# Three 1 MB weight loads in the row stage, each issued in two parts of 120 and 8 partitions

## The reference, cut to what matters

```python
def peer_ffn(x, w_query, sub_keys, expert_u, expert_v):
    def block(xb):                                   # 128 tokens
        q = (xb @ w_query).reshape(128, 8, 2, 128)
        sc = jnp.einsum('thpd,hpkd->thpk', q, sub_keys)
        s_top, i_top = lax.top_k(sc, 16)             # best keys of each half
        ...                                          # best 16 of the 256 sums -> eidx, g = softmax(best)
        u = jnp.take(expert_u, eidx, axis=0)
        h = jax.nn.gelu(jnp.einsum('thkd,td->thk', u, xb))
        vv = jnp.take(expert_v, eidx, axis=0)
        return jnp.einsum('thk,thkd->td', g * h, vv)
```

## Time and profile before

| | |
|---|---|
| median of 3 runs | 1161.68 us (1161.17 to 1161.84) |
| the profiled execution's own time | 1159.69 us |
| its span, first to last instruction | 1157.9 us |
| TensorE busy | 1051.7 us (91%) |
| VectorE busy | 834.9 us (72%) |
| ScalarE busy | 390.7 us (34%) |
| GpSimd busy | 269.4 us (23%) |
| DMA, whole span | 371.86 MB, mean 321 GB/s |
| granted TensorE clock, mean | 0.994 |

### The profile page before, as it was taken

One profiled execution on the slowest core, in us unless ns is written; L12 is line 12 of the kernel. 1 busy time (PEld: TensorE's weight loads), 2 busy tenths in 40 slices (PEclk: granted clock), 3 DMA queues, 4 the chain that ended last, 5 costly groups with the idle time before them and its releaser, 6 DMA issues.

```text
span 1157.9 us, 11980 instructions
## 1 busy us (share of the span) xinstructions
PE 1051.7 (91%) x4108; PEld 665.7 (57%) x4108; DVE 834.9 (72%) x1747; ACT 390.7 (34%) x724; POOL 269.4 (23%) x261
## 2 busy tenths in 40 slices
PE   8999899998998778798877777889999999999998
PEld 6888464454454333244322222359878778888886
DVE  5788878778877768787787776764565496777743
ACT  7664312211220111311121012044765555444432
POOL 0002444434444334433433343400000000000000
PEclk9999999999999989999999999999999999999999
DMA  9847999999999999999999999977533454555540
GB/s 351 337 167 302 423 421 421 421 421 421 420 420 423 420 422 421 421 414 420 411 421 421 405 423 414 423 282 275 177 138 124 161 193 157 192 183 189 192 164 36
DMA packets 55531, 371.86 MB, mean 321 GB/s; under 512 B 6192, under 2 KB 7344, under 8 KB 12080
## 3 DMA queue, kind: packets, MB, share of 16 engines
q0 software_dynamic: 36864, 268.45, 56.0%
q1 hardware_dynamic: 18608, 102.65, 24.4%
HBM read 370.03 MB, written 1.05 MB: 320 GB/s over the span
## 4 chain that ended last, share of the span: by engine, by line
PE 58%; DMA 30%; DVE 8%; issue 3%; ACT 1%; POOL 1%; SPq 0%; DVEq 0%; POOLq 0%; ACTq 0%
DMA uv<-in_peer_uv,eidx 30%; PE bank L2232 13%; PE bank L1931 9%; PE bank L1933 8%; PE bank L1932 8%; PE bank L2406 6%; PE bank L2003 4%; DVE uv L1548 4%; PE bank L2405 3%; PE bank L1902 1%; DVE diag L1562 1%; PE bank L2121 1%; DMA wraw<-in_in1a 1%; POOL uv L721 1%; DVE xn L1770 0%
## 5 line engine op out<-in xcount | busy, mean ns | idle before, releaser
L2232 PE MATMUL bank<-uv,diag 128*128 128x512 f32 x1024 | 491.8, 609 | 92.7 <-DVE diag L1562 91.3
L1548 DVE SCALAR_TENSOR_TENSOR uv<-uv,xn 128x1024 f32<-128x1024 f32 x256 | 313.6, 1225 | 134.6 <-DMA uv<-in_peer_uv,eidx 132.9
L2232 PEld LDWEIGHTS bank<-uv,diag 128*128 128x128 f32 x1024 | 180.3, 191 | 368.4 <-issue 366.2
L721 POOL DMA_INDIRECT uv<-in_peer_uv,eidx x256 | 269.0, 1051 | 480.0 <-PE bank L2232 358.9
L1265 DVE TENSOR_TENSOR w_lo<-wraw,w_hi 128x2048 fp32r<-128x2048 f32 x69 | 157.8, 2290 | 102.4 <-ACT w_hi L797 102.3
L1008 ACT ACTIVATE chosen<-chosen 128x1 f32<-128x1 f32 x256 | 51.8, 203 | 504.9 <-DVE uv L1548 504.7
L797 ACT CAST w_hi<-wraw 128x2048 fp32r<-128x2048 f32 x69 | 131.5, 1908 | 125.5 <-PE bank L1933 63.1
L2406 PE MATMUL bank<-nT_both,w_hi 128*128 128x512 f32 x320 | 109.6, 397 | 0.0
L1562 DVE TENSOR_SCALAR diag<-const,chosen 128x128 f32<-128x128 f32 x256 | 89.4, 349 | 4.9 <-ACT chosen L1008 4.8
L2405 PE MATMUL bank<-nT_both,w_lo 128*128 128x256 f32 x280 | 78.1, 279 | 0.0
L2406 PEld LDWEIGHTS bank<-nT_both,w_hi 128*128 128x128 f32 x320 | 57.3, 188 | 10.9
(11 more groups left out here) (320 smaller groups left out, 1325.8 us busy)
## 6 DMA issues: line engine op xcount, KB each, us to landing
wraw<-in_ff_in SPq DMA_DIRECT2D x22, 1024.0 KB, 4.8
wraw<-in_ff_out SPq DMA_DIRECT2D x11, 1024.0 KB, 4.9
wraw<-in_query SPq DMA_DIRECT2D x4, 1024.0 KB, 5.3
uv<-in_peer_uv,eidx POOLq DMA_INDIRECT x256, 13.4
wraw<-in_in_q SPq DMA_DIRECT2D x2, 1024.0 KB, 8.9
wraw<-in_in_k SPq DMA_DIRECT2D x2, 1024.0 KB, 9.7
wraw<-in_pool_o SPq DMA_DIRECT2D x2, 1024.0 KB, 4.7
wraw<-in_sb_o SPq DMA_DIRECT2D x2, 1024.0 KB, 4.7
```

Of the source, the lines that this page charges most:

```text
L721: pool.indirect_dma_start(out=uv[:, RING_AT[n % RING], :], out_offset=None, in_=io["peer_uv"], in_offset=bass.IndirectOffsetOnAxis(ap=eidx ...
L1548: nc.vector.scalar_tensor_tensor(out=u, in0=u, scalar=1.0, in1=xn[:, head // PEER_HEADS, :], op0=ALU.mult, op1=ALU.mult, accum_out=hdot[he ...
L2232: mm = nc.tensor.matmul(acc[m][:, :], diag[:, n % RING, :], uv[:, RING_AT[n % RING], D + m * HALF:D + (m + 1) * HALF], start=(n % (ROWS // ...
```

## The change

For the blocks `mem_k`, `mem_v` and `in2_va`, `load_block` issues two DMAs in place of one: partitions 0 to 119, and then partitions 120 to 127. The first part has a semaphore of its own for each block, the second one adds to the slot's semaphore as the whole load did, and `wait_loaded` waits for both. All other loads stay as they are.

```diff
+PARTS_OF = {'mem_k': ((0, 120), (120, 128)), 'mem_v': ((0, 120), (120, 128)), 'in2_va': ((0, 120), (120, 128))}
...
+        part_loaded = {name: sem(f"part_loaded_{name}") for name in PARTS_OF}
...
             b = BLOCK_AT[name]
+            if name in PARTS_OF:
+                eng.wait_ge(part_loaded[name], 16 * (len(PARTS_OF[name]) - 1))
             eng.wait_ge(w_loaded[b % R_SLOTS], 16 * (b // R_SLOTS + 1 - sum(n in PIECED for n in IN_SLOTS[b % R_SLOTS:b:R_SLOTS])))
...
-                sp.dma_start(wraw[:, b % R_SLOTS, :], io[name]).then_inc(w_loaded[b % R_SLOTS], 16)
+                if name in PARTS_OF:
+                    for first, last in PARTS_OF[name]:
+                        ins = sp.dma_start(wraw[first:last, b % R_SLOTS, :], io[name][first:last, :])
+                        ins.then_inc(w_loaded[b % R_SLOTS] if last == P else part_loaded[name], 16)
+                else:
+                    sp.dma_start(wraw[:, b % R_SLOTS, :], io[name]).then_inc(w_loaded[b % R_SLOTS], 16)
```

## The result

1174.82 us (median of 4, 1174.38 to 1175.08) against 1161.43 (1160.03 to 1161.84): ratio 1.0121 with a 95% interval of 1.0109 to 1.0133. The change costs 13.4 us where I had forecast a gain of 6.2; no case that I had listed gives this time.

A forecast was written before the change was run, and what follows sets the result against it. One late DMA engine was taken to bound the row stage, and TensorE what follows. Sparing it three loads gains 4.7 + 2.4 - 0.9 = 6.2 us: 1161.7 to 1155.5, range 1154.0 to 1162.6.

The forecast's parts named there:

- What bounds the kernel: Row stage: one late DMA engine sets its end; TensorE bounds what follows, so what the stage gains is kept.
- 3 x 2.5 = 7.5: Row stage: the three loads cost the late engine 2.5 us each, 8 rows of 0.31 us, 7.5 us in all.
- The price of sparing it: End of the row stage: sparing the late engine gains 4.7 + 2.4 - 0.9 = 6.2 us, within 3.8 and 7.5.
- the next engine's rows: Row stage: the second latest engine gets up to 3 extra rows of 0.31 us, taking 0.9 us off the gain.
- 2.4 us of idling: Row stage, 500 to 757 us: other engines idle for buffers at 417 GB/s instead of 421; 2.4 us would be regained.
- limit of 4.7 us: End of the row stage: the second latest engine stops 4.7 us ahead of the late one and becomes the next bound.
- The sign of being spared: End of the row stage: the one-engine stretch at 27 GB/s shrinks from four microseconds to about one or vanishes.
- That 120 partitions spare the late engine: The three loads: the 120-partition part fills 15 engines and leaves out the late one; 1155.5 us, chance 0.69.
- all four cases: Late engine's cost in the split loads: spared 1155.5 us, unchanged 1161.7, one row more 1162.6, 16 rows a load 1169.2.
- Case C: The three loads: the late engine takes a row of the small part, 9 instead of 8; +0.9 us, 1162.6, chance 0.12.
- The bounds: The three loads: each costs the late engine between 0 and 16 rows; 0 was taken.
- The covers: Readers' second waits on semaphores: over 100 us between load and first read cover them, so they cost nothing.

The follow-up runs named there:

- hardly any of the loads: Against the kernel before, one transfer of 2 partitions replaces each of the three loads and the rest isn't loaded: 1152.85 us, ratio 0.9941.
- three engines loaded: Against the kernel before, each of the three loads is eight transfers of 3 partitions 4 apart, the rest not loaded: 1152.27 us, ratio 0.9936.
- seven engines loaded: Against the kernel before, each of the three loads is eight transfers of 7 partitions 4 apart, the rest not loaded: 1160.41 us, ratio 1.0003.
- stepped: Against the kernel before, the three loads bring only partitions 0 to 63, in eight transfers of 8 partitions 4 apart: 1160.90 us, ratio 1.0008.
- adjacent kernel: Against the kernel before, the three loads bring only partitions 0 to 63, in eight transfers of 8 adjacent partitions: 1179.12 us, ratio 1.0162.

## Why the prediction was wrong

- **What bounds the kernel: right, as far as the runs tell.** One DMA engine, or its way into SBUF, sets the end of the row stage, and what it gains or loses arrives at the end of the kernel. With hardly any of the loads the gain is 7.1 us, where the working had 3 x 2.5 = 7.5.
- **The price of sparing it: right in size.** With three engines loaded and the fourth, late one spared, the time falls by 7.4 us, within the 3.8 to 7.5 I had given; the 6.2 allowed for the next engine's rows and for 2.4 us of idling that would vanish. That idling does not vanish: with hardly any load the rate from 500 to 740 us is still 417 GB/s, and with three engines loaded 419. The term was wrong, and so was the limit of 4.7 us that made it needed: the three engines that stayed loaded didn't become the bound.
- **The sign of being spared: wrong.** The stretch at 27 GB/s was to shrink to about a microsecond or vanish with the gain. With hardly any load it is nearly as long as before, 753 to 757 us, and 7.1 us are gained all the same. So the 4.7 us at the end aren't a lag added up over the stage, from which a load could be subtracted, and the stretch alone tells neither that an engine was spared nor that it wasn't.
- **That 120 partitions spare the late engine: most likely wrong.** I put 0.69 on it with the remark that an odd engine would be at the end. It is, by the runs above, the fourth of those that a short transfer uses. The Trainium skill's rule of the lowest-numbered engines, named in the prediction, makes it number 3, counted from 0, and gives it a share of a part of 120; no run shows this share by itself. The Trainium skill's remark that engines 7 and 15 are usually slower doesn't hold here by the same rule: the kernel with seven engines loaded spares number 7 and takes 1160.41 us.
- **The step that failed** is the sentence "The load then takes 0 rows of the engine left out, 9 of eight engines and 8 of seven", with 0.31 us for each row. It prices a row by the engine that carries it, wherever it is written, and all four cases inherit this. The runs show that which partitions go together in a transfer decides the price: 64 rows a load cost nothing beyond the late engine's share when they are 4 apart (1160.90 us) and 18 us more when they are adjacent (1179.12). In the changed kernel all transfers under way slow down, to 310 and 286 GB/s, and this costs 13.4 us on top of the 7 or so that the 3 MB cost before. Case C, 9 rows on the late engine for 0.9 us, may be true besides; it can't be seen under the 13.4.
- **The bounds.** I had none for a transfer of 120 partitions beside the count of rows, though the prediction says itself that no row shows one. The kernel has loads, gathers, broadcasts and stores, all of 128 partitions; that one kind of transfer is absent from a trace is a reason to take the bound from something coarser. The 1024 KB of a load at half the rate of the gathers would have been 2.5 us more a load for everyone, + 7.5 in sum, and the true value is higher.
- **The covers: right.** Added issues, semaphores and waits cost nothing (two parts by columns: ratio 1.0007).

No kernel that loads all rows beats the one before: to spare the late engine its eight rows must be left out, and a transfer that another engine makes into these partitions wasn't tried alone.

## What to carry to other kernels

While the DMA engines are saturated, load blocks over all 128 partitions and cut them by columns if they must be cut: a cut into runs of adjacent partitions, here 120 and 8, 64 and 64 or 112 and 16, slows everything that is under way, in the changed kernel by some 4.5 us for each MB. Where the queue has room and TensorE is the bound the same cut is free, so its price has to be read in the stage, from GB/s against DMA share: a share at 1.02 with the rate down to 310 is contention, not idleness. And look at the end of a stage in windows of 1 us: a sixteenth of the rate for several microseconds says that one engine ends last. Then only what that engine carries has a price, as long as the transfers don't hinder each other; how long it runs alone isn't what sparing it would bring.

## What the runs showed that I had not expected

Half of a load (64 rows) in eight transfers of 8 adjacent partitions costs more than the whole load in 120 and 8: + 19.2 against + 13.4 us. Leaving out three quarters of the three loads, so that four engines have their 8 rows of each and the others none, changes nothing (ratio 1.0006), and leaving out the fourth engine's 24 rows too is worth 8 us. And transfers whose partitions are 4 apart take SyncE twice as long to issue as adjacent ones, 5.45 us against 2.69 for eight. It is the side of SBUF that decides: with only the rows in HBM 4 apart it is 2.70. The stepped and the adjacent kernel:

```profile
370.58 5.45 SPq L630 DMA_DIRECT2D wraw<-in_mem_k  x8
```

```profile
371.32 2.69 SPq L630 DMA_DIRECT2D wraw<-in_mem_k  x8
```
